# State products of the gated linear attention branch: own head blocks in column halves, chunks 0 and 1 in one step

## The chip, the cores and the metric

One NeuronCore of a Trainium2 chip runs the whole program. The metric is device time in microseconds (us), the median of several executions of the compiled kernel; lower is better. Engines: TensorE (PE, with its weight loads listed apart as PEld), VectorE (DVE), ScalarE (ACT), GpSimd (POOL), and SyncE (SP), which issues most of the DMA. PSUM, where the PE writes, has eight banks of 128 partitions x 512 fp32.

## What is computed

Two transformer blocks on 256 tokens of width 1024. What matters here is one branch of the second block, a recurrent (gated linear attention) branch with 4 heads, key width 64, value width 128, in four chunks of 64 tokens:

```
state_inc = einsum('bnjhd,bnjhe->bnhde', k_s, v)         # per chunk n and head h: [64, 128]
def step(state, xs):
    dec, inc = xs
    return dec[..., None] * state + inc, state
_, states = lax.scan(step, init, (decay, state_inc))      # init is zero
o_inter = einsum('bnihd,bnhde->bnihe', q_d, states)
```

The state ahead of chunk 1 is the increment of chunk 0; those ahead of chunks 2 and 3 are a decayed state plus an increment. The increment of the last chunk is not needed. Beside this branch stands a sparse attention branch (eight units n = 0 to 7, each a query block and a group of heads), and the wide projections of the block.

## The kernel before, in words

Nearly all of the PE's work is weight matrices that come from memory in units of 1 MB through four slots. ScalarE rounds each unit to its high part (`split_hi`, two instructions of 128x1024), VectorE subtracts to get the low part (`split_lo`, two instructions), and the PE multiplies three times per tile of 128 rows (high x high, high x low, low x high). A slot is free again when the PE has used the unit.

The order of all engines is one list of steps that the class `Schedule` writes out; each engine walks through the list and executes the steps that it has a function for, so every engine runs strictly in list order. A PSUM bank is handed on by `use`: the next user of a bank waits on the PE until the last reader of the user before has signalled (`open_bank`). Bank 0 is taken by `bank0` inside `gla`, bank 1 by `aux`.

In the stretch around the change, `run` weaves three generators: `nsa` (the sparse attention), `fill` (the wide projections, 12 matmuls of 512 columns per step), and `gla` (the recurrent branch). After each yield of `nsa` the next step of `fill` and the next of `gla` are appended. The list around the changed steps is, in order, with the engines in brackets that have work in a step:

1. `nsa_t` 0 (PE turns the weights of unit 0; its last transpose goes to bank 1 as `nx`; ACT copies them out), `nsa_e` 1 (ACT exponentials), `split_hi` of weight unit 76 (ACT), a fill step (PE), `split_lo` of weight unit 76 (DVE), which the PE uses four fill steps later;
2. `gla_s` 0 (PE, DVE), then at once `nsa_v` 0 (PE writes bank 1 as `no`; ACT copies the high part out, DVE the low part), a fill step (PE);
3. `gla_t` 0 (PE writes bank 0 and bank 1; DVE masks), `nsa_w` 1 (DVE scales the weights), `nsa_s` 2 (PE, DVE), `split_hi` of unit 77, a fill step, `split_lo` of unit 77;
4. `gla_s` 1 (PE, DVE), then at once `nsa_t` 1 (PE), `nsa_e` 2 (ACT), a fill step, `nsa_v` 1, `split_hi` of unit 78, a fill step, `split_lo` of unit 78, `gla_o` 0 (PE, ACT), and so on;
5. later `split_lo` of unit 79, `gla_s` 2, at once `nsa_v` 2 (PE), a fill step, `gla_t` 1.

`gla_s` (PE, lines 1710 to 1721; DVE, lines 3003 to 3019) makes the state. The PE multiplies, for each pair of heads c, 64 tokens x 128 keys (two heads) by 64 tokens x 256 values (two heads): a 128x256 result, of which only the two blocks of a head with itself are used. VectorE copies the four 64x128 blocks (n = 0) or folds them into the decayed state with four scalar_tensor_tensor instructions (n = 1, 2). Its PE matmuls read KB and VB, which live in the tile AR, and are recorded at the helper line 1318; DVE copies are recorded at line 2462, scalar_tensor_tensor at 2459, tensor_tensor at 2451, ACT copies at 1944; transposes at 1332. An fp32 matmul leaves two records in the trace, so `gla_s` shows as x4 and `nsa_v` 0 as x12.

`STATE[1]` and `STATE[2]` lie where the tile EL was, `STATE[3]` where XC was; in these the two pairs of heads c stand beside each other, head 2c + h in partition half h.

Of the kernel before, what the change touches and what calls it, by code (L numbers as in the profile page):

```python
# [11 lines left out]
ALU = mybir.AluOpType  # L12
# [121 lines left out]
class Schedule:  # L134
# [590 lines left out]
    def gla(self):  # L725
        def bank0(key):
            return self.use(key, [0])

        bank0(("gk",))
        self.step("gla_k")  # L730
        yield
        bank0(("gs", 0))
        self.step("gla_s", n=0)
        yield
        yield from self.gla_scores(0, bank0)
        bank0(("gs", 1))
        self.step("gla_s", n=1)
        yield
        yield
        yield from self.gla_sums(0, bank0)  # L740
        self.step("gla_n", i=0)
        yield
        bank0(("gs", 2))
        self.step("gla_s", n=2)
        yield
        yield from self.gla_scores(1, bank0)
        yield
        yield
        yield from self.gla_sums(1, bank0)
        self.step("gla_n", i=1)  # L750
        yield
        self.step("gla_r")
        yield
        yield
        yield
        for i in range(2):
            bank0(("gT", i))
            self.step("gla_T", i=i)
            yield
# [265 lines left out]
def two_blocks(nc, A, out):  # L1025
    ctx = ExitStack()
    with ctx:
# [55 lines left out]
        def ar(off, *shape):  # L1083
            return part(AR, 18432, off, shape)
# [12 lines left out]
        def bank(use):  # L1097
            return PS[:, use.banks[0], :]

        def halves(ap):  # L1100
            return ap.rearrange("p (a n) -> p a n", a=2)
# [39 lines left out]
        KB = ar(4608, 2, 256)  # L1141
        EB = ar(5120, 2, 256)
# [3 lines left out]
        VB = ar(6656, 2, 512)  # L1146
# [17 lines left out]
        STATE = [None, EL[:, 0, :].rearrange("p (a e) -> p a e", a=2),  # L1164
                 EL[:, 1, :].rearrange("p (a e) -> p a e", a=2),
                 XC[:, 0, :].rearrange("p (a e) -> p a e", a=2)]
# [71 lines left out]
        U = S.U  # L1238
# [75 lines left out]
        def tensor_program(eng):  # L1314
            pe = Engine(eng)

            def mm(o, l, r, start, stop):
                return nc.tensor.matmul(o, l, r, start=start, stop=stop, skip_group_check=True)  # L1318
# [15 lines left out]
            def open_bank(use):  # L1334
                for w in use.after:
                    pe.wait_ge(*w)
# [371 lines left out]
                m.then_inc(use.full[0], 1)  # L1708

            def gla_s(s):  # L1710
                n = s["n"]
                lo = 64 * (n % 2)
                use = U["gs", n]
                pe.wait_ge(*U["gk",].read)
                for i in range(2):
                    pe.wait_ge(*U["vb", 0, i].read)
                open_bank(use)
                for c in range(2):
                    m = mm(bank(use)[:, 256 * c:256 * c + 256], KB[lo:lo + 64, n // 2, 128 * c:128 * c + 128],
                           VB[lo:lo + 64, n // 2, 256 * c:256 * c + 256], True, True)  # L1720
                m.then_inc(use.full[0], 1)

            def gla_t(s):
                i = s["i"]
# [190 lines left out]
            def up2_m(s):  # L1915
# [4 lines left out]
                if h == 1:  # L1920
# [4 lines left out]
                       "pool_o": pool_o, "merge_t": merge_t, "tiles": tiles, "rows": rows, "end_rows": end_rows, "mem_t": mem_t, "mix_turn": mix_turn, "kv": kv,  # L1925
                       "small": small, "cmp_m": cmp_m, "cmp_t": cmp_t, "cmp_o": cmp_o, "gat": gat, "al": al,
                       "gla_a": gla_a, "gla_k": gla_k, "gla_s": gla_s, "gla_t": gla_t, "gla_o": gla_o,
                       "gla_T": gla_T, "nsa_s": nsa_s, "nsa_t": nsa_t, "nsa_v": nsa_v, "xat_s": xat_s,
                       "xat_t": xat_t, "xat_v": xat_v, "ffn_turn": ffn_turn, "upt_high": upt_high, "upt_low": upt_low,
# [516 lines left out]
        def vector_program(eng):  # L2446
            dve = Engine(eng)
# [10 lines left out]
            def stt(o, a, c, b, op0, op1):  # L2458
                return nc.vector.scalar_tensor_tensor(o, a, c, b, op0, op1)  # L2459

            def cp(o, a):
                return nc.vector.tensor_copy(o, a)
# [538 lines left out]
                tt(EL[:], EL[:], KB[:], ALU.mult).then_inc(s_gel, 1)  # L3001

            def gla_s(s):
                n = s["n"]
                use = U["gs", n]
                dve.wait_ge(*use.full)
                if n > 0:
                    dve.wait_ge(*U["gs", n - 1].read)
                    dve.wait_ge(s_zc, 2)
                for c in range(2):  # L3010
                    for h in range(2):
                        rr = slice(64 * h, 64 * h + 64)
                        o = STATE[n + 1][rr, c, :]
                        inc = bank(use)[rr, 256 * c + 128 * h:256 * c + 128 * h + 128]
                        if n == 0:
                            m = cp(o, inc)
                        else:
                            m = stt(o, STATE[n][rr, c, :], EB[rr, c, 64 * n + 63:64 * n + 64], inc, ALU.mult, ALU.add)
                m.then_inc(use.read[0], 1)

            def gla_t(s):
                i = s["i"]
# [210 lines left out]
            def final2(s):  # L3233
# [11 lines left out]
                       "raw_inverse": raw_inverse, "rows": rows, "end_rows": end_rows, "mem_norm": mem_norm, "mem_t": mem_t,  # L3245
                       "final1": final1, "kv": kv, "small": small, "cmp_z": cmp_z, "cmp_h": cmp_h, "cmp_g": cmp_g, "cmp_t": cmp_t,
                       "cmp_o": cmp_o, "gat": gat, "al": al, "gla_a": gla_a, "gla_c": gla_c, "gla_m": gla_m, "gla_s": gla_s,
                       "gla_t": gla_t, "gla_n": gla_n, "gla_r": gla_r, "gla_T": gla_T, "nsa_s": nsa_s, "nsa_w": nsa_w,
                       "nsa_v": nsa_v, "mix_turn": mix_turn, "xat_s": xat_s, "xat_w": xat_w, "xat_v": xat_v, "ffn_gain": ffn_gain, "ffn_inverse": ffn_inverse, "ffn_scaled": ffn_scaled,
# [188 lines left out]
```

## Time and profile before

| | |
|---|---|
| median of 3 runs | 821.45 us (821.12 to 821.71) |
| profiled execution: its time, its span | 821.45 us, 819.6 us |
| PE busy | 804.7 us (98%) |
| DVE busy | 609.3 us (74%) |
| ACT busy | 453.5 us (55%) |
| POOL busy | 96.5 us (12%) |
| DMA | 143.40 MB, 175 GB/s on average |

The profile is one execution recorded by the hardware profiler. Its span is the time from the first to the last instruction; the execution's time is 1.8 us longer. The engines run side by side, so a busy share alone says little: what matters is which engine's wait ends last at a place. Matmuls are pipelined, and their recorded durations overlap; the distance from start to start is what one costs in a row. A figure in brackets behind a row of the timeline is the idle time of the engine ahead of it and what ended it ("issue" is time in which the engine waited for nothing that the profile shows).

### The profile page before, as it was taken

What the parts mean: (1) busy time and instruction counts of PE and PEld (TensorE: products, weight loads), DVE (VectorE), ACT (ScalarE), POOL (GpSimd) and SP (SyncE); (2) the same over time, 40 slices, a digit from 0 to 9 for tenths busy, and PEclk for the clock granted to TensorE, in tenths of its full rate; (3) what the DMA queues carried; (4) which work ended last, traced back from release to release, by engine and by line L of the source; (5) the groups of instructions that cost most, each with busy time, mean ns of one, the idle gap of its engine ahead of it and who ended that gap; (6) DMA issues with size and microseconds to landing.
All of it is one profiled execution on the core that took longest, in us unless ns stands there. A gap on an engine that the chain in (4) does not pass through costs nothing.

```text
span 819.6 us, 12095 instructions
## 1 busy us (share of the span) xinstructions
PE 804.7 (98%) x4841; PEld 697.8 (85%) x4841; DVE 609.3 (74%) x967; ACT 453.5 (55%) x804; POOL 96.5 (12%) x106
## 2 busy tenths in 40 slices
PE   7999999999999999999999999999999999999997
PEld 6878888888888888889998778788888999999886
DVE  6878776978777855567669777958577799998734
ACT  6656556645545634445475656664387655554533
POOL 4100000000000000000400000000000555654100
PEclk9999999999999999999999999999999999999999
DMA  9854644556665555554966343365633555555551
GB/s 326 239 162 152 197 150 154 162 173 192 224 201 180 182 203 183 177 205 114 258 203 206 104 129 130 103 154 180 203 106 115 194 170 190 185 176 196 180 189 51
DMA packets 81640, 143.40 MB, mean 175 GB/s; under 512 B 5123, under 2 KB 35873, under 8 KB 81585
## 3 DMA queue, kind: packets, MB, share of 16 engines
q1 hardware_dynamic: 79264, 137.11, 51.5%
q0 software_dynamic: 2160, 5.46, 2.3%
q8 instruction: 38, 0.62, 0.3%
q14 instruction: 18, 0.14, 0.1%
q10 hardware_dynamic: 160, 0.07, 0.0%
HBM read 141.05 MB, written 1.05 MB: 173 GB/s over the span
## 4 chain that ended last, share of the span: by engine, by line
PE 92%; DVE 4%; ACT 3%; issue 0%; DMA 0%; ACTq 0%; DVEq 0%
PE PS L1318 89%; PE PS L1332 3%; ACT WK_f L1941 1%; DVE low_r L2451 1%; ACT high L1944 1%; DMA VR<-in_norm_attn_g_dram 0%; ACT WK_f L1944 0%; DVE WK_f L2455 0%; DVE WK_f L2459 0%; DVE XN L2451 0%; DVE XN L2459 0%; DVE HT_r L2451 0%; DVE AR_f L2459 0%; ACT L1938 0%; DVE X L2451 0%
## 5 line engine op out<-in xcount | busy, mean ns | idle before, releaser
L2451 DVE TENSOR_TENSOR low_r<-low_f,high 128x1024 fp32r<-128x1024 f32 (+1 forms) x256 | 325.8, 1315 | 75.8 <-ACT high L1944 75.4
L1944 ACT ACTIVATE high<-low_f 128x1024 fp32r<-128x1024 f32 (+1 forms) x264 | 257.3, 1024 | 78.6 <-DMA low_f<-in_w_down_dram 34.8
L1318 PE MATMUL PS<-HT_r,high 128*128 128x256 f32 (+2 forms) x1232 | 267.5, 308 | 0.0
L1318 PE MATMUL PS<-high,AR_r 128*128 128x512 f32 (+2 forms) x724 | 214.7, 377 | 0.0
L1318 PEld LDWEIGHTS PS<-HT_r,high 128*128 128x128 f32 (+1 forms) x1232 | 199.6, 190 | 12.3
L1318 PE MATMUL PS<-HT_r,low_r 128*128 128x256 f32 (+1 forms) x712 | 200.9, 282 | 0.0
L1318 PE MATMUL PS<-high,HT_r 128*128 128x512 f32 (+1 forms) x576 | 189.6, 397 | 1.0 <-DVE HT_r L2451 0.7
L1318 PEld LDWEIGHTS PS<-high,AR_r 128*128 128x128 f32 (+1 forms) x724 | 129.1, 181 | 26.3 <-issue 0.5
L1318 PEld LDWEIGHTS PS<-HT_r,low_r 128*128 128x128 f32 (+1 forms) x712 | 135.2, 190 | 0.0
L1318 PE MATMUL PS<-low_r,AR_r 128*128 128x512 f32 (+2 forms) x362 | 133.9, 374 | 0.0
L1318 PEld LDWEIGHTS PS<-high,HT_r 128*128 128x128 f32 x576 | 108.2, 190 | 25.4 <-issue 2.7
L1318 PE MATMUL PS<-low_r,HT_r 128*128 128x512 f32 (+1 forms) x288 | 110.9, 387 | 0.0
L1318 PEld LDWEIGHTS PS<-low_r,AR_r 128*128 128x128 f32 (+1 forms) x362 | 65.5, 181 | 12.2
L3258 POOL TENSOR_TENSOR WK_f<-WK_f 128x512 f32<-128x512 f32 x33 | 53.3, 1616 | 115.1 <-DVE WK_f L2459 113.3
L1318 PEld LDWEIGHTS PS<-low_r,HT_r 128*128 128x128 f32 x288 | 54.9, 190 | 9.3
L1944 ACT ACTIVATE AR_r<-AR_f 128x512 fp32r<-128x512 f32 (+1 forms) x29 | 18.1, 629 | 69.4 <-DVE AR_f L2451 38.5
L2451 DVE TENSOR_TENSOR AR_r<-AR_f,AR_r 128x512 fp32r<-128x512 f32 (+1 forms) x29 | 23.7, 821 | 18.9 <-ACT AR_r L1944 18.9
L1941 ACT ACTIVATE WK_f<-WK_f,st 128x128 f32<-128x128 f32 (+2 forms) x80 | 33.0, 416 | 6.0 <-DVE st L2455 6.0
L1318 PE MATMUL PS<-AR_f 64*128 64x128 f32 (+5 forms) x268 | 30.3, 317 | 0.7 <-DVE AR_r L2451 0.6
L1318 PEld LDWEIGHTS PS<-AR_f 64*128 64x128 f32 (+2 forms) x268 | 23.8, 182 | 8.5 <-issue 5.6
L1944 ACT ACTIVATE WK_f<-PS 128x512 f32<-128x512 f32 (+2 forms) x38 | 15.3, 448 | 28.2 <-PE PS L1332 25.3
L1944 ACT ACTIVATE AR_f<-PS 128x512 f32<-128x512 f32 (+2 forms) x34 | 18.7, 550 | 21.8 <-PE PS L1318 20.3
(174 smaller groups left out, 675.8 us busy)
## 6 DMA issues: line engine op xcount, KB each, us to landing
low_f<-in_w_in_dram SPq DMA_DIRECT2D x39, 1024.0 KB, 5.2
low_f<-in_w_up_dram SPq DMA_DIRECT2D x38, 1024.0 KB, 5.2
low_f<-in_w_down_dram SPq DMA_DIRECT2D x27, 1024.0 KB, 4.9
low_f<-in_w_out_dram SPq DMA_DIRECT2D x8, 1024.0 KB, 5.0
low_f<-in_w_xkv_dram SPq DMA_DIRECT2D x4, 1024.0 KB, 5.6
low_f<-in_w_branch_gla_dram SPq DMA_DIRECT2D x2, 1024.0 KB, 5.0
low_f<-in_w_branch_nsa_dram SPq DMA_DIRECT2D x4, 512.0 KB, 6.0
low_f<-in_w_xq_dram SPq DMA_DIRECT2D x2, 1024.0 KB, 5.2
```

What stands on the lines that cost most here:

```text
L1318: return nc.tensor.matmul(o, l, r, start=start, stop=stop, skip_group_check=True)
L1332: return nc.tensor.transpose(o, i, ident[0:n, 0:n])
L1941: return nc.scalar.activation(o, i, f, bias=bias, scale=scale, accum_out=total)
L1944: return nc.scalar.activation(o, i, ACT.Copy, bias=0.0, scale=1.0)
L2451: return nc.vector.tensor_tensor(o, a, b, op)
L3258: return nc.gpsimd.tensor_tensor(o, a, b, op)
```

## The change

In the list of steps, `gla_s` 0 becomes one step for the chunks 0 and 1, whose two products go to bank 0 and bank 1; the step `gla_s` 1 goes away, its yield stays. `gla_s` 2 stays in its place. On the PE each step now multiplies, per head and chunk, 64 tokens x 64 keys by 64 tokens x 128 values, the two heads of a pair into the two column halves of the array and, in the first step, the two chunks from the two row halves. On VectorE the result of a chunk lies in one 128x256 block: one copy for chunk 0, and two scalar_tensor_tensor of 128x128 for the chunks 1 and 2.

```diff
         bank0(("gs", 0))
-        self.step("gla_s", n=0)
+        self.aux(("gs", 1))
+        self.step("gla_s", ns=(0, 1))
         yield
         yield from self.gla_scores(0, bank0)
-        bank0(("gs", 1))
-        self.step("gla_s", n=1)
         yield
         yield
         yield from self.gla_sums(0, bank0)
         self.step("gla_n", i=0)
         yield
         bank0(("gs", 2))
-        self.step("gla_s", n=2)
+        self.step("gla_s", ns=(2,))
...
             def gla_s(s):
-                n = s["n"]
-                lo = 64 * (n % 2)
-                use = U["gs", n]
                 pe.wait_ge(*U["gk",].read)
                 for i in range(2):
                     pe.wait_ge(*U["vb", 0, i].read)
-                open_bank(use)
+                for n in s["ns"]:
+                    open_bank(U["gs", n])
                 for c in range(2):
-                    m = mm(bank(use)[:, 256 * c:256 * c + 256], KB[lo:lo + 64, n // 2, 128 * c:128 * c + 128],
-                           VB[lo:lo + 64, n // 2, 256 * c:256 * c + 256], True, True)
-                m.then_inc(use.full[0], 1)
+                    for h in range(2):
+                        for n in s["ns"]:
+                            use = U["gs", n]
+                            lo, at = 64 * (n % 2), 128 * c + 64 * h
+                            m = mm(bank(use)[64 * h:64 * h + 64, 128 * c:128 * c + 128],
+                                   KB[lo:lo + 64, n // 2, at:at + 64],
+                                   VB[lo:lo + 64, n // 2, 2 * at:2 * at + 128], True, True)
+                            if c == h == 1:
+                                m.then_inc(use.full[0], 1)
...
             def gla_s(s):
-                n = s["n"]
-                use = U["gs", n]
-                dve.wait_ge(*use.full)
-                if n > 0:
+                for n in s["ns"]:
+                    use = U["gs", n]
+                    inc = halves(bank(use)[:, 0:256])
+                    dve.wait_ge(*use.full)
+                    if n == 0:
+                        cp(STATE[1], inc).then_inc(use.read[0], 1)
+                        continue
                     dve.wait_ge(*U["gs", n - 1].read)
                     dve.wait_ge(s_zc, 2)
-                for c in range(2):
-                    for h in range(2):
-                        rr = slice(64 * h, 64 * h + 64)
-                        o = STATE[n + 1][rr, c, :]
-                        inc = bank(use)[rr, 256 * c + 128 * h:256 * c + 128 * h + 128]
-                        if n == 0:
-                            m = cp(o, inc)
-                        else:
-                            m = stt(o, STATE[n][rr, c, :], EB[rr, c, 64 * n + 63:64 * n + 64], inc, ALU.mult, ALU.add)
-                m.then_inc(use.read[0], 1)
+                    for c in range(2):
+                        m = stt(STATE[n + 1][:, c, :], STATE[n][:, c, :], EB[:, c, 64 * n + 63:64 * n + 64], inc[:, c, :],
+                                ALU.mult, ALU.add)
+                    m.then_inc(use.read[0], 1)
```

## Rows read from the trace of the kernel before

**Rows 1.** The page: granted TensorE clock in 40 slices, chain that ended last by engine.

```profile
PEclk9999999999999999999999999999999999999999
...
PE 92%; DVE 4%; ACT 3%; issue 0%; DMA 0%; ACTq 0%; DVEq 0%
```

**Rows 2.** Timeline of PE from 457 to 469 us: start us, us, engine line op.

```profile
457.31 0.39 PE L1318 MATMUL PS<-high,HT_r 128*128 128x512 f32 x1
457.63 1.13 PE L1318 MATMUL PS<-AR_f 64*128 64x256 f32 x4
458.69 0.88 PE L1318 MATMUL PS<-WK_f,AR_f 128*64 128x128 f32 x12
459.49 0.50 PE L1318 MATMUL PS<-high,HT_r 128*128 128x512 f32 x1
...
462.12 0.39 PE L1318 MATMUL PS<-high,HT_r 128*128 128x512 f32 x1
462.85 1.29 PE L1318 MATMUL PS<-AR_f 64*128 64x128 f32 x20 [0.34 <-DVE AR_r L2451]
...
467.01 1.13 PE L1318 MATMUL PS<-AR_f 64*128 64x256 f32 x4
468.07 0.77 PE L1332 MATMUL PS<-cst,WK_f 128*128 128x128 f32 x5
```

**Rows 3.** Timeline of DVE from 458 to 469 us.

```profile
458.91 2.36 DVE L2451 TENSOR_TENSOR low_r<-low_f,high 128x1024 fp32r<-128x1024 f32 x2 [2.65 <-ACT high L1944]
461.19 1.19 DVE L2462 COPY AR_f<-PS 64x128 f32<-64x128 f32 x4
462.41 0.29 DVE L2451 TENSOR_TENSOR AR_r<-PS,AR_r 128x128 fp32r<-128x128 f32 x1
...
466.60 0.91 DVE L2459 SCALAR_TENSOR_TENSOR WK_f<-cst,PS 128x15 f32<-128x15 f32 x4
```

**Rows 4.** Timeline of ACT from 457 to 460 us.

```profile
457.84 1.99 ACT L1944 ACTIVATE high<-low_f 128x1024 fp32r<-128x1024 f32 x2
459.73 0.26 ACT L1944 ACTIVATE AR_r<-PS 128x128 fp32r<-128x128 f32 x1
```

**Rows 5.** Groups of instructions by line and shape (count, busy us, mean ns), whole span.

```profile
L2462 DVE COPY AR_f<-PS 128x256 f32<-128x256 f32 x11 | 4.6, 420 | 0.8 <-PE PS L1318 0.7
```

**Rows 6.** Line 2459 from 487.05 to 488.4 us: duration ns min/median/max, first to last start.

```profile
L2459 DVE SCALAR_TENSOR_TENSOR AR_f<-AR_f,PS x4: 332/346/353, 487.0 to 488.1; 64x128 f32<-64x128 f32 x4
```

**Rows 7.** Timeline of PE from 453 to 455 us.

```profile
454.23 0.74 PE L1332 MATMUL PS<-cst,WK_f 128*128 128x128 f32 x5 [0.54 <-DVE WK_f L2459]
```

**Rows 8.** Timeline of DVE from 453 to 455 us.

```profile
453.84 0.90 DVE L2459 SCALAR_TENSOR_TENSOR WK_f<-cst,PS 128x15 f32<-128x15 f32 x4
```

**Rows 9.** Timeline of PE from 483 to 489 us.

```profile
483.78 1.13 PE L1318 MATMUL PS<-AR_f 64*128 64x256 f32 x4
...
488.27 0.39 PE L1318 MATMUL PS<-high,HT_r 128*128 128x512 f32 x1
488.88 1.71 PE L1318 MATMUL PS<-AR_f 64*128 64x128 f32 x20 [0.22 <-DVE AR_r L2451]
```

**Rows 10.** Timeline of DVE from 486 to 489 us.

```profile
486.99 1.42 DVE L2459 SCALAR_TENSOR_TENSOR AR_f<-AR_f,PS 64x128 f32<-64x128 f32 x4
488.44 0.29 DVE L2451 TENSOR_TENSOR AR_r<-PS,AR_r 128x128 fp32r<-128x128 f32 x1
```

**Rows 11.** Timeline of PE from 0 to 16 us.

```profile
4.47 0.24 PE L1332 MATMUL PS<-cst,VR 8*128 8x8 f32 x1 [4.47 <-DMA VR<-in_norm_attn_g_dram]
...
10.07 1.06 PE L1318 MATMUL PS<-high,HT_r 128*128 128x512 f32 x2
...
13.49 0.48 PE L1318 MATMUL PS<-low_r,HT_r 128*128 128x512 f32 x1
...
15.19 0.62 PE L1318 MATMUL PS<-high,HT_r 128*128 128x512 f32 x2
```

## The prediction

> **What bounds the kernel now.** I read the page first: the granted TensorE clock and the chain that ended last. The chain is PE for 92% of the span [rows 1]. So time is saved or lost only where the PE works less or waits more, and the question for each edit is whether it changes the PE's queue or something that the PE waits for. Then I read the PE's timeline around the changed steps [rows 2]. The row at 457.63 us is `gla_s` 0 (x4 is two matmuls), the next one starts 1.06 us later and is `nsa_v` 0; at 459.49 the wide projection goes on. `gla_s` 1 stands at 467.01 and again costs 1.06 (until 468.07); `gla_s` 2 is at 483.78 [rows 9]. The PE waits for nothing ahead of any of these three. Third, VectorE over the same stretch [rows 3], because it frees the banks: at 457.63 it is idle, then it does the split of weight unit 76 from 458.91 to 461.27, then the four copies of `gla_s` 0 from 461.19 to 462.38, then the low part of `nsa_v` 0. The split comes ahead of the copies in list order and can't start sooner: ScalarE rounds that unit from 457.84 [rows 4]. So the chunk-0 product lies in bank 0 for some 3 us before VectorE looks at it. Before the change that costs nothing, as bank 0 isn't wanted until `gla_t` 0 at 462.85.
>
> **The change part by part.** Times are on the clock of the profiled execution, 821.45 us with a span of 819.6; that execution is also the median of the three runs, so differences carry over unchanged.
>
> *Chunk 1 goes to bank 1, at `gla_s` 0.* This is the new wait. Bank 1 is next written by `nsa_v` 0, which follows `gla_s` 0 at once on the PE. Before, `nsa_v` 0 needed only that ScalarE had read `nx` 0. Now it needs VectorE to have read the chunk-1 product, and VectorE reaches `gla_s` only behind the split. Release: VectorE starts at 461.19 as before [rows 3]; one copy of 128x256 from PSUM is 0.42 [rows 5], to 461.61; then two scalar_tensor_tensor, which I price by the ones of `gla_s` 2: starts 0.36 apart and 0.35 long [rows 6] (the new ones have 128 partitions instead of 64 and as many elements in each), so 0.71, to 462.33. From the end of a VectorE read to the PE's start is 0.15: the read at 462.41 is 0.29 long and the PE starts at 462.85 [rows 2, 3]. `nsa_v` 0 starts at about 462.5 instead of 458.69: the PE is **+3.8 us** late, of which about 4.1 us is idle time behind the shorter new `gla_s`. How long the eight new matmuls take does not enter, since they end before 458.7 at the slowest I expect, over 2 us ahead of VectorE. Bounds: nothing, if VectorE freed the bank before the PE comes to it; above, if the merged instructions cost as much as the eight old ones (1.19 and 1.42, [rows 3, 10]) the release is 463.8 + 0.15 and the delay 5.3. I take 3.8, because start and durations are both rows of the same place.
>
> Queued behind the waiting PE is everything, so all later PE work moves by this much. ScalarE stands at its part of `nsa_v` 0 (459.73, [rows 4]) and its next split, of unit 77, moves with it; VectorE takes that one only behind its work at 466.60 [rows 3], so it is not late.
>
> *`gla_t` 0.* It waited for VectorE's low part of `nsa_v` 0. The last fill matmul starts at 462.12; from the last fill matmul to such an fp32 group is 0.32 where nothing is waited for (457.31 to 457.63), so without the wait it would start at 462.44, not 462.85 [rows 2]. After the change VectorE has nothing ahead of that low part, and it is done over 1 us before the PE comes: **-0.4 us**.
>
> *`gla_s` 1 is gone from its old place.* The PE goes from the fill to `nsa_t` 1 directly: **-1.06 us** [rows 2]. What is late next is `nsa_t` 1's banks and weights, which VectorE frees in `nsa_s` 2. By the same step one unit before, the PE starts 0.39 after the VectorE group begins (453.84 to 454.23, [rows 7, 8]). So the group at 466.60 allows 466.99 [rows 3], and the PE would come at 467.01 [rows 2]: it just fits, with both sides moved alike by the delay. I count no loss; the bound is the whole 1.06. VectorE also loses 1.42 us of work there, which nobody waits for.
>
> *`gla_s` 2 with narrow tiles.* Before 1.06. `nsa_v` 0 is six matmuls of 128 columns in alternating column halves and costs 0.80 from start to start [rows 2], two thirds of that for four matmuls is 0.53; with a little for the change of tile shape I take 0.6: **-0.45 us**. Bounds: 0 (four in a row, 128 columns each, are as many columns as two of 256) and -0.55.
>
> *`gla_t` 1.* The last fill matmul starts at 488.27, so it could start at 488.59 and starts at 488.88, waiting for VectorE's low part of `nsa_v` 2 at 488.44 [rows 9, 10]. VectorE's four scalar_tensor_tensor (1.42) become two (0.71), the low part comes at 487.7 and is readable by 488.15; the PE now comes at 488.14: **-0.3 us**.
>
> *The other edits*: the four copies that become one are counted in the release; fewer semaphore signals cost nothing visible.
>
> Sum: 3.8 - 0.4 - 1.06 - 0.45 - 0.3 = **+1.6 us**, 821.45 + 1.6 = 823.05, say 823.1. About 0.2% (1.64 us) is what a measurement of this kernel can tell from no change; the forecast lies on that edge.
>
> The page TensorEngine Tiling of the Trainium skill, section Performance Considerations (PSUM Bottleneck), speaks against the change: tiling makes the matmuls faster and leaves reading PSUM as it was, so the read may become the limit. By that rule alone the sum would be a loss at the merged step and no more than the tile gain elsewhere; the rows above say the same, with the read's place in VectorE's queue, not its length, as the larger part.
>
> **Rivals.**
>
> *The clock falls in the new gap.* The PE has no idle time longer than the 4.47 us at the start, where its matmuls are then slow: a pair of 512 columns shows as 1.06 us at 10.07 against 0.62 at 15.19, and the row at 13.49 is the first in between [rows 11]. That is the lower level, 1.2 GHz, though the page's granted clock shows 9 tenths or more in every slice [rows 1]. The new gap of about 4.1 us is nearly as long. If the clock falls there, the PE runs at half speed for some 4 us afterwards (at the start the slow rows go from 10.07 or sooner to about 13.5) and loses about 2: 825.1. Against it: the start is the first work of all, and no gap inside the kernel is long enough to show. The page TensorE: Matmul & The Clock Gate (Part 1) says that idle time gates the clock down to half and renewed work releases it; no row here shows it in the middle of the kernel.
>
> *`nsa_t` 1 meets a wait.* The PE comes to it 1.06 us sooner and the margin is 0.02. If VectorE is later by as much as it may, the 1.06 is not gained: up to 824.1.
>
> *Faster: VectorE frees bank 1 in time.* The price of everything hangs on whether VectorE does `gla_s` behind the split. If it had read chunk 1 by 460.9 (a delay of 2.2 instead of 3.8) the change would be even; if ahead of the split, there is no delay, and the sum is -1.06 - 0.45 - 0.3 and some 0.2 for a shorter first step: 819.4. Against: the split is ahead in list order, and it waits for ScalarE, which finishes the exponentials of `nsa_e` 1 only at 457.84 [rows 4]. No row speaks for it except that the split's start is set by ScalarE and could shift.
>
> **How the numbers follow.** Forecast 0.62, its own range 822.4 to 823.8 (release 0.3 either way, `gla_s` 2 at 0 to -0.55). Clock 0.22, at 824 to 826. Wait at `nsa_t` 1 0.09. Faster 0.07. The range leaves out most of the faster case and the top of the clock case: 822.0 to 825.6. The forecast splits about evenly over the 0.2% edge, the clock and the wait cases are slower: slower 0.6, same 0.33, faster 0.07.
>
> **What would show it.** In the PE's timeline a `gla_s` row of x16 at 457.6, then an idle time of 3.8 to 4.2 us that ends at a VectorE read of line 2459, ahead of the x12 row of `nsa_v` 0. On VectorE one copy 128x256 and two scalar_tensor_tensor 128x128 behind the split of unit 76. No wait at `gla_t` 0 or `gla_t` 1; `nsa_t` 1 directly behind the fill, with less than 0.1 idle. `gla_s` 2 as x8 in about 0.6. With the clock rival, pairs of 512 columns of 1.06 instead of 0.62 behind the gap. It would be wrong if there is no such gap, or if the time moved by more than 3 us without slow matmuls.

## The result and the profile after

| | before | changed |
|---|---|---|
| median of 6 runs each, one chip | 821.44 us (821.12 to 821.71) | 824.86 us (823.97 to 825.16) |
| ratio, 95% interval | | 1.0048 [1.0038, 1.0059] |
| span of the profiled execution | 819.6 us | 823.4 us |
| PE busy | 804.7 us | 804.9 us |
| mean granted TensorE clock | 1.000 | 0.995 |

The change makes the kernel slower by 3.4 us, twice what the forecast (823.1) said, and inside the range. Slower was the forecast's side, but the size is that of the first rival, whose price was 825.1. The profiled execution, 825.16 us, is at the long end of its six.

First the timeline of PE around the merged step, in the changed kernel (the rows that answer to [rows 2]; the bracket is the idle time ahead of the row and what ended it; the helper lines stand a few lines off, 1317 for 1318 and 2462 for 2459):

```profile
457.46 0.39 PE L1317 MATMUL PS<-high,HT_r 128*128 128x512 f32 x1
457.78 0.67 PE L1317 MATMUL PS<-AR_f 64*64 64x128 f32 x16
...
462.62 1.55 PE L1317 MATMUL PS<-WK_f,AR_f 128*64 128x128 f32 x12 [4.18 <-DVE AR_f L2462]
464.10 0.80 PE L1317 MATMUL PS<-high,HT_r 128*128 128x512 f32 x1
...
465.12 1.05 PE L1317 MATMUL PS<-high,HT_r 128*128 128x512 f32 x2
...
467.48 0.63 PE L1317 MATMUL PS<-high,HT_r 128*128 128x512 f32 x2
...
468.50 1.29 PE L1317 MATMUL PS<-AR_f 64*128 64x128 f32 x20
...
472.68 0.74 PE L1331 MATMUL PS<-cst,WK_f 128*128 128x128 f32 x5
```

The x16 row is `gla_s` for both chunks: eight matmuls, where the two of before took 1.13. Then PE is idle for 4.18 us until a VectorE scalar_tensor_tensor ends. What comes behind the gap is new too: the twelve records of `nsa_v` 0 take 1.48 us from start to start (462.62 to 464.10) where they took 0.80, and a pair of wide matmuls is 1.05 long at 465.12 and 0.63 at 467.48. The granted clock names the cause. The next view has a stretch of 5 us per line: its length, the busy time of PE, PEld, DVE, ACT and POOL (with the number of instructions), the granted clock as a share of 2.4 GHz, the DMA share and GB/s:

```profile
455.00:460.00 5.00, 3.45 (x30) 2.45 (x28) 2.31 (x4) 4.76 (x17) 0.00 (x0) 1.00 0.53 194
460.00:465.00 5.00, 2.38 (x14) 1.98 (x15) 2.66 (x6) 0.79 (x2) 0.00 (x0) 0.54 0.00 0
465.00:470.00 5.00, 5.00 (x32) 3.91 (x32) 0.75 (x2) 1.38 (x2) 0.00 (x0) 0.78 0.10 11
470.00:475.00 5.00, 5.00 (x25) 3.95 (x25) 4.79 (x20) 2.13 (x9) 0.00 (x0) 1.00 0.55 198
```

0.54 and 0.78 are means over five microseconds of the two levels, 2.4 and 1.2 GHz (1.00 and 0.50); around them it is 1.00. Third, VectorE over the same time, to see why the gap ends where it does (answers to [rows 3]):

```profile
459.06 2.36 DVE L2454 TENSOR_TENSOR low_r<-low_f,high 128x1024 fp32r<-128x1024 f32 x2 [2.65 <-ACT high L1947]
461.34 0.42 DVE L2465 COPY AR_f<-PS 128x256 f32<-128x256 f32 x1
461.87 0.61 DVE L2462 SCALAR_TENSOR_TENSOR AR_f<-AR_f,PS 128x128 f32<-128x128 f32 x2
464.52 0.29 DVE L2454 TENSOR_TENSOR AR_r<-PS,AR_r 128x128 fp32r<-128x128 f32 x1 [2.04 <-ACT AR_r L1947]
```

The split of weight unit 76 is first, then the copy of chunk 0 and the two instructions of chunk 1. Reading the two products takes 1.1 us; 2.3 us of the gap are the split ahead of them, and 0.6 us pass before the split starts (it waits for ScalarE's rounding). Last, the second place, `gla_s` 2 and `gla_t` 1 (answers to [rows 9]):

```profile
488.38 0.65 PE L1317 MATMUL PS<-AR_f 64*64 64x128 f32 x8
488.96 0.88 PE L1317 MATMUL PS<-WK_f,AR_f 128*64 128x128 f32 x12
...
492.71 1.71 PE L1317 MATMUL PS<-AR_f 64*128 64x128 f32 x20
```

`gla_s` 2 costs 0.58 from start to start instead of 1.06, and `gla_t` 1 has no idle time ahead of it any more.

### The profile page after: what moved, and what is told of

Same layout as the page of the kernel before. It is cut to its first block, busy times and chain, and to the rows that moved or that the text cites. A ratio compares the mean times of both kernels' runs of the same rounds, so it can differ in the third digit from the quotient of the medians.

```text
span 823.4 us, 12113 instructions
## 1 busy us (share of the span) xinstructions
PE 804.9 (98%) x4853; PEld 697.8 (85%) x4853; DVE 606.9 (74%) x960; ACT 453.5 (55%) x804; POOL 96.5 (12%) x106
## 3 DMA queue, kind: packets, MB, share of 16 engines
HBM read 141.05 MB, written 1.05 MB: 173 GB/s over the span
## 4 chain that ended last, share of the span: by engine, by line
PE 93%; DVE 3%; ACT 2%; issue 0%; DMA 0%; DVEq 0%; ACTq 0%
PE PS L1317 90%; PE PS L1331 3%; ACT WK_f L1944 1%; DVE low_r L2454 1%; ACT high L1947 1%; DMA VR<-in_norm_attn_g_dram 0%; DVE WK_f L2458 0%; DVE WK_f L2462 0%; DVE XN L2454 0%; DVE XN L2462 0%; DVE HT_r L2454 0%; ACT WK_f L1947 0%; ACT L1941 0%; DVE X L2454 0%; ACT AR_f L1947 0%
## 5 line engine op out<-in xcount | busy, mean ns | idle before, releaser
L1317 PE MATMUL PS<-AR_f 64*128 64x128 f32 (+5 forms) x280 | 28.3, 310 | 0.2 <-ACT AR_f L1947 0.2
```

## The experiments

A single execution of this program is uncertain by about as much as most of the edits here are worth: the kernel before ran from 819.93 to 821.72 us over the 50 executions beside the experiments. So each experiment is read twice, by its median and by the position of its steps in its trace. In the table, "shift" is the time from the start of `gla_s` 0 to the start of `gla_t` 1, less the 31.25 us that it takes in the kernel before (457.63 to 488.88, [rows 2, 9]). The medians are against the kernel before, run beside it on the same chip. In ten of the eleven traces the time from `gla_t` 1 to the end of the span is 330.6 to 330.9 us (330.7 before), so nothing outside the shift and the start of the program differs by more than 0.3 us; the exception is e3, below.

| kernel | idle ahead of `nsa_v` 0 | `nsa_v` 0 to `gla_t` 0 | shift | median, against before | ratio, 95% |
|---|---|---|---|---|---|
| before | 0 | 4.16 | 0 | | |
| changed | 4.18 | 5.88 | +3.68 | +3.42 | 1.0048 [1.0038, 1.0059] |
| changed, again (e8) | 4.17 | 5.35 | +3.14 | +3.08 | 1.0036 [1.0021, 1.005] |
| three fillers (e7) | 3.28 | 5.34 | +3.11 | +3.83 | 1.0038 [1.0023, 1.0053] |
| eight fillers (e1) | 2.15 | 3.75 | +1.54 | +2.70 | 1.0034 [1.002, 1.0047] |
| twelve fillers (e9) | 1.24 | 3.77 | +1.58 | +1.58 | 1.002 [1.0011, 1.0029] |
| wait alone (e2) | 3.77 | 6.06 | +5.75 | +5.51 | 1.0067 [1.0052, 1.0082] |
| tiles alone (e3) | 0 | 3.75 | -2.09 | -1.54 | 0.9981 [0.9972, 0.9991] |
| chunk 1 in bank 4 (e4) | 0 | 4.43 | -2.07 | -1.71 | 0.998 [0.997, 0.999] |
| VectorE reads first (e5) | 1.34 | 3.76 | -1.28 | -1.09 | 0.9984 [0.9974, 0.9993] |
| both of these (e6) | 0 | 3.88 | -2.63 | -2.32 | 0.9968 [0.9955, 0.9981] |

The third column is 3.75 when nothing waits and the clock is full; what is clearly above it is the clock in the rows with idle time of 3.28 us or more, and the wait at `gla_t` 0 in those of before, e4 and e6.

**Fill the gap, keep the wait (e1).** The wait for bank 1 stays, but the PE gets eight matmuls that nobody reads, into bank 4, between `gla_s` and it (`FILLERS` is 8). The wait for `U["ns", 1]` only makes sure that bank 4 has been read.

```diff
                             if c == h == 1:
                                 m.then_inc(use.full[0], 1)
+                if 0 in s["ns"]:
+                    pe.wait_ge(*U["ns", 1].read)
+                    for _ in range(FILLERS):
+                        mm(PS[:, 4, :], HT.hi[:, 0, 0:128], HTP[:, 0, :, :].rearrange("p a n -> p (a n)"), True, True)
```

> The changed kernel with eight matmuls of 512 columns (TensorE work whose result nobody reads, into bank 4) between the first gla_s and nsa_v 0, so that the wait for bank 1 stays but TensorE is idle for only some 2.4 us of it. Theory A (the gap makes the clock fall, and that costs 2.1 us of its own): nsa_v 0 starts at the same place, about 3.8 us late, but its 12 records take 0.80 us and the next fill step 2.95, granted clock 1.00 from 460 to 470 us; the time falls by 2.1 to about 822.8. Rival B (the slow stretch comes with the 64x64 tiles or with the wait as such, not with idle time): nsa_v 0 still takes 1.5 us, the fill step 4.4, and the time stays at 824.9.

PE timeline of this kernel:

```profile
457.99 2.10 PE L1318 MATMUL PS<-HT_r 128*128 128x512 f32 x8
462.25 0.88 PE L1318 MATMUL PS<-WK_f,AR_f 128*64 128x128 f32 x12 [2.15 <-DVE AR_f L2467]
463.06 0.50 PE L1318 MATMUL PS<-high,HT_r 128*128 128x512 f32 x1
```

`nsa_v` 0 starts 4.86 us behind the start of `gla_s` 0, as in the changed kernel (4.84), but at full clock: 0.81 to the next step. The shift is +1.54 against +3.68. So tile shape and wait are those of the changed kernel, only the idle time is different, and the slow stretch is gone: rival B falls. The median, 2.70 over the kernel before (interval +1.6 to +3.9), is above what this one trace shows, and two of the five executions had a mean clock of 0.997, which none of the kernel before has. The fall may have happened in some of them; no trace shows it, and so one trace without a fall does not make a gap of 2.15 us safe. Hence e9.

**Twelve fillers (e9)**, the same kernel with `FILLERS = 12`.

> As the run with the filled gap, with twelve matmuls instead of eight: TensorE is idle for some 1.3 us ahead of nsa_v 0. With eight the profiled execution kept its clock and its steps moved by +1.5, but the median was +2.7 over the kernel before, with granted clocks down to 0.997, so the clock may have fallen in some executions. Theory A: with so short a gap it falls in none, the mean granted clock of every execution is 0.998 or more, as in the kernel before, and the median is +1.6 (from +1.2 to +2.0). Rival F (a loss beside wait and clock that the stretch around the step does not show): +2.3 or more at a clock of 0.998 to 1.000.

The shift is +1.58 and the median +1.58; the mean clock is 0.998 or 0.999 in all eleven executions. This is the forecast's sum, 1.6, measured (interval of the median: +0.9 to +2.4). No third loss (rival F) shows.

**Three fillers (e7)**, `FILLERS = 3`.

> As the run with the filled gap, with three matmuls of 512 columns instead of eight, which leaves TensorE idle for some 3.3 us. Gaps of 3.8 and 4.2 us made the clock fall, one of 2.2 did not. Theory A says only that the time is one of two: about +1.6 over the kernel before with the clock at 1.00, or about +3.6 with slow matmuls for some 4 us behind the gap; a value in between for a single execution would speak against a clock that has two levels here.

The gap is 3.28 us and the clock falls, but at another place. PE timeline of this kernel:

```profile
462.08 0.88 PE L1318 MATMUL PS<-WK_f,AR_f 128*64 128x128 f32 x12 [3.28 <-DVE AR_f L2467]
462.89 0.50 PE L1318 MATMUL PS<-high,HT_r 128*128 128x512 f32 x1
463.22 0.44 PE L1318 MATMUL PS<-low_r,HT_r 128*128 128x512 f32 x1
463.46 1.05 PE L1318 MATMUL PS<-high,HT_r 128*128 128x512 f32 x2
...
466.02 1.01 PE L1318 MATMUL PS<-high,HT_r 128*128 128x512 f32 x2
466.87 0.40 PE L1318 MATMUL PS<-low_r,HT_r 128*128 128x512 f32 x1
```

`nsa_v` 0 and the first wide matmuls run at full speed; the clock falls about 1.4 us after work has begun again and is back at 466.8. The loss is 1.6 us (5.34 less 3.75), the shift +3.11. By the expectation's last sentence that is "in between" (+1.6 or +3.6), which I had said would speak against two levels. It does not: the rows show two durations, 1.05 and 0.63; it is the stretch of work that falls on the lower level that varies. My expectation was too narrow there. The median does not separate this kernel from the changed one: +3.83 here and +3.08 in e8, with intervals that overlap.

**The changed kernel again (e8).**

> The changed kernel as it is, beside the others on one chip. Theory A: 3.4 to 3.8 us over the kernel before, 2.1 over the one with the filled gap (whose idle time was 2.2), with nsa_v 0 at 1.48 us from start to start and its next fill step at 4.4.

The median is +3.08, the shift +3.14, with the gap at 4.17 us; 3.4 to 3.8 was expected. Here too the expected detail was wrong: `nsa_v` 0 ran at full speed (its row is 0.88 long) and the slow part came later, worth 1.60 us. So the same program with the same gap loses 2.1 us in one execution and 1.6 in another.

**The wait alone, in the kernel before (e2).**

```diff
                 pe.wait_ge(*U["co", 1].read)
                 open_bank(use)
+                if n == 0:
+                    pe.wait_ge(*U["gs", 0].read)
```

> The kernel before, with one wait more: nsa_v 0 on TensorE also waits until VectorE has read the chunk-0 product. No tile, bank or step is changed. Theory A: nsa_v 0 starts at about 462.5 instead of 458.7 (+3.8), the wait at gla_t 0 goes (-0.4), and if the clock falls in a gap of 3.8 us another +2.1 comes: 821.4 + 3.4 = 824.8, or 826.9 with the clock. Rival B (the 64x64 tiles are what slows TensorE down): +3.4 without slow matmuls, whatever the length of the gap. Rival C (the delay of one step is made up later by engines that have caught up): under 823.

PE timeline of this kernel:

```profile
457.30 1.13 PE L1318 MATMUL PS<-AR_f 64*128 64x256 f32 x4
462.20 1.55 PE L1318 MATMUL PS<-WK_f,AR_f 128*64 128x128 f32 x12 [3.77 <-DVE AR_f L2464]
468.26 1.29 PE L1318 MATMUL PS<-AR_f 64*128 64x128 f32 x20
```

The median is +5.51, as theory A had it (+5.5 with the clock). With old tiles and old banks the same slow rows come behind the gap. So this wait, with the fall of the clock behind it, makes the loss of the change, and it is not made up later: rival C, under 823, falls at 826.23.

**The tiles alone (e3).** The narrow matmuls and merged VectorE instructions of the change, with chunk 0 and 1 in their old steps and bank 0.

```diff
-        self.aux(("gs", 1))
-        self.step("gla_s", ns=(0, 1))
+        self.step("gla_s", ns=(0,))
         yield
         yield from self.gla_scores(0, bank0)
+        bank0(("gs", 1))
+        self.step("gla_s", ns=(1,))
```

> The narrow tiles and the merged VectorE instructions alone: chunk 0 and chunk 1 keep their own steps and bank 0, as before the change. Theory A: no new wait, clock 1.00 throughout. gla_s 1 and gla_s 2 take 0.58 instead of 1.06 each (-0.96), the wait at gla_t 1 goes (-0.3); what gla_s 0 saves on TensorE is lost in the wait at gla_t 0 unless VectorE's shorter copies (-0.75) bring that forward (-0.4 and up to -0.5 more): about 819.5, between 819.0 and 820.2. Rival B (64x64 tiles cost clock or a drain): no faster than 821.4.

Median -1.54, shift -2.09: this half of the change is a gain by itself. Each `gla_s` is x8 and takes 0.58 on the PE, and the waits at `gla_t` 0 and 1 are gone. The median is 0.5 us less of a gain than the shift. In this trace the time from `gla_t` 1 to the end of the span is 331.45 us, 0.7 more than in the kernel before; 0.4 of it is one slow pair of wide matmuls at 758.04 us (1.03 long) with no idle time ahead of it. Its cause, and whether it comes in the other executions, is open.

**Chunk 1 in bank 4 (e4).**

```diff
-        self.aux(("gs", 1))
+        self.use(("gs", 1), [4])
```

> The changed kernel with the chunk-1 product in bank 4 instead of bank 1; bank 4 is next written by nsa_s 2, behind gla_t 0. Theory A (the whole loss is that bank 1 is wanted at once): nsa_v 0 follows the first gla_s directly, the clock stays at 1.00, and of the parts of the sum the gains stay: step gone -1.06, gla_s 2 -0.48, gla_t 1 -0.3, first step no gain because gla_t 0 still waits: 821.4 - 1.8 = 819.6. Rival D (the step for two chunks itself, two row halves and two banks at once, is slow or VectorE's merged work is late): 821 or more, with a wait of over 0.5 us at nsa_s 2.

PE timeline of this kernel:

```profile
456.58 0.67 PE L1317 MATMUL PS<-AR_f 64*64 64x128 f32 x16
457.18 0.88 PE L1317 MATMUL PS<-WK_f,AR_f 128*64 128x128 f32 x12
461.61 1.29 PE L1317 MATMUL PS<-AR_f 64*128 64x128 f32 x20 [0.61 <-DVE AR_r L2454]
```

Nothing waits at `nsa_v` 0, and no wait shows behind `gla_t` 0 either, so rival D falls (819.01 us). The merged step with its eight matmuls costs 0.60 us, two hundredths more than four matmuls in e3: so the two row halves do work side by side. But merging gains next to nothing over e3 (-2.07 against -2.09), because the PE's gain of 0.58 from the step that is gone is given back at `gla_t` 0, which waits 0.61 us for VectorE.

**VectorE reads first (e5)** and **both (e6)**. The VectorE part of the merged step is a step of its own, `gla_early`, put into the list ahead of the split of unit 76; PE's part stays where it was. e6 has bank 4 too.

```diff
         self.step("gla_s", ns=(0, 1))
+        at = max(k for k, s in enumerate(self.steps) if s.name == "split_lo")
+        self.steps.insert(at, Step("gla_early", 0, {"ns": (0, 1)}))
...
             def gla_s(s):
+                if 0 not in s["ns"]:
+                    gla_early(s)
+
+            def gla_early(s):
                 for n in s["ns"]:
```

> The changed kernel with one thing moved: on VectorE the reading of both chunk products comes ahead of the split of weight unit 76 instead of behind it; TensorE's and ScalarE's order, the banks and the wait stay. Theory A (the wait is long only because the read stands behind the split in VectorE's queue): TensorE waits some 1.3 us at nsa_v 0 instead of 4.2, nsa_v 0 starts 1.0 us later than before the change instead of 3.8, no slow matmuls; the sum is +1.0 - 0.4 - 1.04 - 0.48 - 0.3 = -1.2 against the kernel before, so 3.6 us under the changed kernel run beside it. Rival E (what TensorE waits for is the length of VectorE's read or the semaphore): the gap stays over 3 us.

> Chunk 1 in bank 4 and VectorE's read ahead of the split. Theory A: no wait at nsa_v 0; the wait at gla_t 0 (0.6 us with bank 4 alone) shrinks to some 0.2, since the split now ends 0.5 later than the copies did but nothing stands between it and the low part of nsa_v 0: 2.0 to 2.3 us under the kernel before, the fastest so far. Rival: the split of unit 76 or the next one comes late for TensorE, and the time is that of bank 4 alone (-1.7) or more.

VectorE's timeline in e5:

```profile
457.42 0.42 DVE L2467 COPY AR_f<-PS 128x256 f32<-128x256 f32 x1 [2.09 <-PE PS L1319]
457.96 0.61 DVE L2464 SCALAR_TENSOR_TENSOR AR_f<-AR_f,PS 128x128 f32<-128x128 f32 x2
458.48 2.35 DVE L2456 TENSOR_TENSOR low_r<-low_f,high 128x1024 fp32r<-128x1024 f32 x2
```

In e5 the PE waits 1.34 us instead of 4.18, though bank 1 and the wait are those of the changed kernel, and the sign turns: -1.09 by the median, -1.28 by the shift, -1.2 expected. Rival E falls; the place of the read in VectorE's queue is what made the gap. e6 is the fastest of all kernels here: 817.82 us against 820.14, ratio 0.9968 [0.9955, 0.9981], and beats both the kernel before and the changed one (about 5.4 us under e8 on the same chip).

## Why the prediction was right and where it was wrong

The range held the time and the direction was right. The likeliest case was not the one that happened: the forecast was the sum without the clock, and the rival "The clock falls in the new gap", given 0.22, came true. The forecast's own range, 822.4 to 823.8, missed 824.86; the stated range held it only because it was drawn around the clock case as well.

- *Chunk 1 goes to bank 1: +3.8.* Measured +3.78: `nsa_v` 0 starts 4.84 us behind `gla_s` 0 instead of 1.06. The release worked out from VectorE's queue was right to 0.03 us; the copy took 0.42 as priced, the pair 0.61 instead of 0.71, but 0.11 lay idle between the copy and it.
- *`gla_t` 0: -0.4.* With full clock the third column of the table falls from 4.16 to 3.75 (e1): -0.41.
- *`gla_s` 1 gone: -1.06.* From `gla_t` 0 to `nsa_t` 1 it is 4.18 in the changed kernel (468.50 to 472.68) against 5.22 before: -1.04. The margin of 0.02 at `nsa_t` 1 held to 0.02, and that rival fell.
- *`gla_s` 2: -0.45.* Measured 0.58 against 1.06: -0.48.
- *`gla_t` 1: -0.3.* 3.75 from `nsa_v` 2 (488.96 to 492.71) against 4.04 (484.84 to 488.88; 484.84 is 483.78 + 1.06): -0.29.
- *Sum: +1.6.* The kernel with the wait but with only 1.24 us of idle time (e9) gives +1.58, by the median and by the trace.

The step that failed is the clock case's chance. The prediction argued that "no gap inside the kernel is long enough to show" a fall and took that for a reason against it. It was no evidence either way: the longest idle time that the kernel before has behind the start is 1.53 us. All four profiled executions with a gap of 3.28 us or more (changed, e2, e7, e8) show the fall, and the price was right: 2 forecast, 2.1 in the profiled execution, 1.6 in e8. With the clock case as the forecast the time would have been 825.1 against 824.86 measured. The page TensorE: Matmul & The Clock Gate of the Trainium skill (Part 1), cited beside the rival, says that idle time halves the clock. The rows here agree for the four gaps of 3.28 to 4.18 us, and show no fall behind those of 1.24, 1.34 and 2.15 us in one trace each. The page TensorEngine Tiling of the Trainium skill (Performance Considerations, PSUM Bottleneck) pointed at the right place, a read of PSUM that the PE comes to wait for, but the trace does not bear out its reason. The reads did not stay as they were: chunk 0's went from 1.19 to 0.42 us, and the two products together take 1.1 us of the 4.18. Moving them in VectorE's queue alone (e5) turned the loss into a gain.

The rival on the faster side named its mechanism rightly (VectorE frees bank 1 ahead of the split) and could not happen in the kernel as given; e5 is that rival made true. Its price was too good: it had no delay at all and 819.4, 2.0 under the kernel before. In e5 `nsa_v` 0 still starts 0.95 us late (2.01 behind `gla_s` 0 instead of 1.06), because VectorE's reads end 1.87 us behind the start of `gla_s` 0 (458.57 less 456.70), where the old step was over after 1.06; the gain is 1.1 to 1.3. The sign changes where that rival says, at a delay of 2.2, but its time for the read, 460.9, is the PE's start; the read would have to end 0.15 sooner.

## What to carry to other kernels

When a result is moved to another bank, look up who writes that bank next and where the read that frees it stands in the reader's queue: here a read of 1.1 us held the bottleneck engine for 4.2 us, because it stood behind a split whose result was wanted only four fill steps later. In this kernel an idle time of TensorE of 3.3 to 4.2 us cost itself plus another 1.6 to 2.3 us at half clock; other work put into it (e9) took the second part away. And judge the parts of a change apart: the narrow tiles were worth 2 us by the shift and 1.5 by the median (e3), and the merged step nothing more until VectorE's order was changed too (e6, 0.5 us ahead of e3 by the shift; e3 itself has no wait left there that another order could take away).

## What was not expected of the hardware

The clock need not fall in the gap; it can fall after work has begun again. In e7 the rows are at full speed for 1.4 us behind a gap of 3.28 us, and only then slow, for 3.4 us (463.46 to 466.87); in the profiled execution of the change they are slow from the first one, from 462.62 to about 467.2. The granted clock in steps of 1 us shows both. The changed kernel, where it falls inside the gap (458.4 to 462.6):

```profile
460.00:461.00 1.00, 0.00 (x0) 0.00 (x0) 1.00 (x2) 0.00 (x0) 0.00 (x0) 0.71 0.00 0
461.00:462.00 1.00, 0.00 (x0) 0.00 (x0) 0.89 (x3) 0.00 (x0) 0.00 (x0) 0.50 0.00 0
```

The same program in e8, where the gap ends at 461.21 and the clock falls behind it:

```profile
461.00:462.00 1.00, 0.79 (x12) 0.66 (x12) 0.06 (x1) 0.00 (x0) 0.00 (x0) 1.00 0.00 0
462.00:463.00 1.00, 1.00 (x5) 0.79 (x4) 0.29 (x1) 0.88 (x2) 0.00 (x0) 0.60 0.00 0
```

The cost was 2.13 (changed), 1.60 (e8), 1.59 (e7) and 2.31 us (e2) in the four traces (third column less 3.75); it is the larger one in the two, changed and e2, where the work behind the gap is slow from its first row.

The start of the program differs from execution to execution in the same way. The change's profiled execution has pairs of wide matmuls that are 1.05 long at 10.11 and 11.39 us and 0.90 at 12.67, and that of e8, the same program, has none at all:

```profile
9.09 0.80 PE L1317 MATMUL PS<-high,HT_r 128*128 128x512 f32 x1 [0.49 <-DVE HT_r L2454]
10.11 1.05 PE L1317 MATMUL PS<-high,HT_r 128*128 128x512 f32 x2
11.39 1.05 PE L1317 MATMUL PS<-high,HT_r 128*128 128x512 f32 x2
```

```profile
9.07 0.50 PE L1317 MATMUL PS<-high,HT_r 128*128 128x512 f32 x1 [0.61 <-DVE HT_r L2454]
9.65 0.62 PE L1317 MATMUL PS<-high,HT_r 128*128 128x512 f32 x2
10.34 0.62 PE L1317 MATMUL PS<-high,HT_r 128*128 128x512 f32 x2
```

`gla_s` 0 then starts at 457.78 in the first and at 456.37 in the second, 1.4 us apart in the same program. All eleven traces follow this: `gla_s` 0 starts at 456.18 to 456.58 in the four without slow pairs at the start (e4, e6, e8, e9), at 456.70 in e5, which has one, and at 457.24 to 457.78 in the six with more. That this also makes the spread of the kernel before (819.93 to 821.72) is likely but not shown, as only one of its executions has a trace (821.45 us, with slow pairs). The profile's granted clock is 1.00 over the first 15 us in all eleven, so a slow start has to be read from the durations. For edits worth 1 or 2 us, positions against a step just ahead of the edit are the sharper measure.

The other surprise is how cheap the quadrants are: eight fp32 matmuls of 128 columns in 64x64 tiles over both row halves took 0.60 us from start to start (e4), four over one row half 0.58 (e3), and the two of 256 columns in 64x128 tiles, which four of them replace, 1.06.
